# mLSTM blocks in transposed form: the gate maximum by a scan along tokens, its rows by transposing a repeated column

## The reference, cut to what matters

```python
b = jnp.cumsum(logf, axis=-1)
D = jnp.where(causal, b[..., :, None] - b[..., None, :] + logi[..., None, :], -jnp.inf)
inter = b + m[..., None]
m_t = jnp.maximum(inter, jnp.max(D, axis=-1))
w_inter = jnp.exp(inter - m_t)
S = jnp.einsum('bhtd,bhsd->bhts', q, k) * jnp.exp(D - m_t[..., None])
num = w_inter[..., None] * jnp.einsum('bhvk,bhtk->bhtv', C, q) + jnp.einsum('bhts,bhsv->bhtv', S, v)
den = w_inter * jnp.einsum('bhk,bhtk->bht', n, q) + jnp.sum(S, axis=-1)
```

## Time and profile before

| | |
|---|---|
| median of 3 runs | 2477.17 us (2476.88 to 2477.39) |
| profiled execution, its span | 2478.2 us (its time is known by the span alone) |
| PE busy | 2446.6 us |
| DVE busy | 1588.2 us |
| ACT busy | 1096.2 us |
| POOL busy | 527.5 us |
| granted TensorE clock, mean | 0.997 of full speed |
| mixer of layer 0, L1068 of block 0 to L1145 of block 8 | 191.7 to 448.1 us |
| mixer of layer 1, the same | 1410.2 to 1670.1 us |

### The profile page before, as it was taken

How to read it: one execution, slowest core, us unless ns; L and a number is a source line. 1 busy time by engine, 2 the same in 40 slices (tenths; PEclk the granted TensorE clock), 3 DMA queues, 4 the chain that set the end, 5 groups by cost and what they waited for, 6 DMA issues and landing times.

```text
span 2478.2 us, 41945 instructions
## 1 busy us (share of the span) xinstructions
PE 2446.6 (99%) x16611; PEld 2381.6 (96%) x16611; DVE 1588.2 (64%) x2693; ACT 1096.2 (44%) x2067; POOL 527.5 (21%) x490
## 2 busy tenths in 40 slices
PE   9999999999999999999999999999999999999999
PEld 8999888999999999999999988889999999999999
DVE  3115688878888887465611266878888888864564
ACT  6326656534333333343433355645334333343453
POOL 0001253423222220010110112433322222200110
PEclk9999999999999999999999999999999999999999
DMA  4442322122222223554525333212222222155564
GB/s 153 132 133 92 115 84 77 54 70 65 75 79 70 79 77 110 191 175 160 190 71 155 110 97 115 82 49 71 66 75 79 70 79 77 63 167 169 176 195 146
DMA packets 238072, 265.89 MB, mean 107 GB/s; under 512 B 15639, under 2 KB 207925, under 8 KB 235701
## 3 DMA queue, kind: packets, MB, share of 16 engines
q1 hardware_dynamic: 237876, 263.22, 33.5%
HBM read 213.06 MB, written 50.11 MB: 106 GB/s over the span
## 4 chain that ended last, share of the span: by engine, by line
PE 87%; DVE 6%; issue 3%; ACT 2%; DMA 1%; POOL 0%; SPq 0%; DVEq 0%; POOLq 0%; ACTq 0%
PE bank L323 27%; PE bank L325 26%; PE bank L324 26%; PE bank L1119 1%; PE bank L1046 1%; DMA zb<-z_scratch 1%; PE bank L1104 1%; PE bank L1088 1%; DVE actL L2265 1%; PE bank L1129 1%; PE bank L1068 1%; DVE hc L2201 0%; PE bank L1080 0%; DMA rawB<-in_w_down 0%; PE bank L999 0%
## 5 line engine op out<-in xcount | busy, mean ns | idle before, releaser
L323 PE MATMUL bank<-actH,wb 128*128 128x384 f32 (+1 forms) x1712 | 560.4, 327 | 1.8 <-DVE xT L2062 1.8
L324 PE MATMUL bank<-actL,wb 128*128 128x384 f32 (+1 forms) x1712 | 554.8, 324 | 0.0
L325 PE MATMUL bank<-actH,wb 128*128 128x384 f32 (+1 forms) x1712 | 554.4, 324 | 0.0
L323 PE MATMUL bank<-wzH,actH 128*128 128x256 f32 (+3 forms) x1296 | 369.1, 285 | 3.2 <-DVE wzL L2019 2.1
L325 PE MATMUL bank<-wzH,actL 128*128 128x256 f32 (+3 forms) x1296 | 364.2, 281 | 0.0
L324 PE MATMUL bank<-wzL,actH 128*128 128x256 f32 (+3 forms) x1296 | 363.8, 281 | 0.0
L323 PEld LDWEIGHTS bank<-actH,wb 128*128 128x128 f32 x1712 | 322.4, 188 | 7.2 <-issue 6.2
L324 PEld LDWEIGHTS bank<-actL,wb 128*128 128x128 f32 x1712 | 323.1, 189 | 0.7
L325 PEld LDWEIGHTS bank<-actH,wb 128*128 128x128 f32 x1712 | 323.2, 189 | 0.0
L323 PEld LDWEIGHTS bank<-wzH,actH 128*128 128x128 f32 (+1 forms) x1296 | 236.3, 182 | 6.1 <-issue 4.0
L323 PE MATMUL bank<-tH,wb 128*128 128x384 f32 x704 | 237.0, 337 | 1.2 <-ACT vn L1817 1.2
(11 more groups left out here) (311 smaller groups left out, 5152.5 us busy)
## 6 DMA issues: line engine op xcount, KB each, us to landing
raw<-in_w_up SPq DMA_DIRECT2D x88, 512.0 KB, 4.4
raw<-in_w_down SPq DMA_DIRECT2D x88, 512.0 KB, 3.6
g_scratch<-cv SPq DMA_DIRECT2D x44, 545.0 KB, 3.2
rawz<-in_w_in SPq DMA_DIRECT2D x22, 1024.0 KB, 5.4
zb<-z_scratch SPq DMA_DIRECT2D x16, 1156.0 KB, 5.4
tHf<-g_scratch SPq DMA_DIRECT2D x88, 192.0 KB, 3.7
z_scratch<-zst SPq DMA_DIRECT2D x128, 128.0 KB, 1.7
raw<-in_w_out SPq DMA_DIRECT2D x128, 128.0 KB, 2.8
```

The lines of the kernel that those rows point to most:

```text
L323: pe.matmul(out, aH, bH, start=first, stop=False)
L324: pe.matmul(out, aH, bL, start=False, stop=False)
L325: return pe.matmul(out, aL, bH, start=False, stop=last)
```

## The change

The mask is now that of the upper triangle, and Am, the weights and the scores stand as (s, t) instead of (t, s). The running maximum of a is no longer a reduction of a masked 128x512 matrix: PE transposes aa to four rows (`gate_rows`), DVE scans them along the tokens (`run`), PE transposes the result back to a column (`gate_columns`, between the two halves of the scores of nx), and DVE takes the maximum with mp (`gate_top`, behind the reciprocal and ahead of hc). In the next block PE spreads M_t over the partitions by transposing the column cm repeated 128 times, four transposes in place of the matmul of dA. DVE's subtraction makes mask minus M_t, ACT adds a_s as the bias of four exponentials, and the product with q by k gives WTs at once: Wt, its transposes on PE and their copy on ACT go, and so do dA on POOL and the two reductions and the subtraction on DVE.

```diff
-    t[:, CM:CM + P] = np.where(np.tril(np.ones((P, P))) > 0, 0.0, -BIG)
+    t[:, CM:CM + P] = np.where(np.triu(np.ones((P, P))) > 0, 0.0, -BIG)
...
+                def gate_rows(nx):
+                    par, i, zi, r, kind = nx
+                    pe.wait_ge(S["aa_r"], l * 9 + i + 1)
+                    if kind == "sample":
+                        pe.wait_ge(cn_r, l * 2 + 2)
+                    small(r)
+                    pe.transpose(bank[3][0:4, 8:8 + r], aa[0:r, :], ident[0:r, 0:r]).then_inc(S["aT_r"], 1)
+                def gate_columns(nx):
+                    par, i, zi, r, kind = nx
+                    pe.wait_ge(S["run_r"], l * 9 + i + 1)
+                    small(r)
+                    pe.transpose(bank[3][0:r, 136:140], run[0:4, 0:r], ident[0:4, 0:4]).then_inc(S["top_r"], 1)
...
                         if c:
-                            pe.wait_ge(S["bb_r"], b1)
+                            gate_columns(nx)
                             settle(pe, settled)
                         for p in range(4):
+                            if c and p == 2:
+                                pe.wait_ge(S["cm_r"], b1)
...
+                    if kind == "sample":
+                        gate_columns(nx)
...
-                    pe.wait_ge(S["dA_r"], b1)
+                    pe.wait_ge(S["cm_r"], b1)
...
-                    pe.matmul(bank[6][:, 0:4 * r], ones[0:r, :], dA[0:r, 0:4 * r], start=True, stop=True).then_inc(S["A_r"], 1)
+                    for h in range(4):
+                        m = pe.transpose(bank[6][:, h * P:h * P + r], cm[0:r, h:h + 1].broadcast_to([r, P]), ident[0:r, 0:r])
+                    m.then_inc(S["A_r"], 1)
...
-                        m = pe.matmul(bank[6][0:r, h * P:h * P + r], qz[:, h, 0:r], ckT[:, h // 2, 0:r],
+                        m = pe.matmul(bank[6][0:r, h * P:h * P + r], ckT[:, h // 2, 0:r], qz[:, h, 0:r],
...
-                    pe.wait_ge(S["W_r"], b1)
-                    small(r)
-                    for h in range(4):
-                        m = pe.transpose(bank[6][0:r, h * P:h * P + r], Wt[0:r, h, 0:r], ident[0:r, 0:r])
-                    m.then_inc(S["WT_r"], 1)
...
                         pe.matmul(bank[6][0:r, h * 65:h * 65 + 65], WTs[0:r, h, 0:r], Vx[0:r, h, :], start=True, stop=True)
+                    if nx is not None:
+                        gate_rows(nx)
...
+                    act.wait_ge(S["D_r"], b1)
+                    for h in range(4):
+                        t = act.activation(Am[0:r, h, 0:r], Am[0:r, h, 0:r], ACT.Exp, bias=aa[0:r, h:h + 1])
+                    t.then_inc(S["P_r"], 1)
                     act.wait_ge(S["sm_r"], b1)
                     act.activation(ex[:, :], sm[:, :], ACT.Exp).then_inc(S["ex_r"], 1)
-                    act.wait_ge(S["D_r"], b1)
-                    act.activation(Am[0:r, :, 0:r], Am[0:r, :, 0:r], ACT.Exp).then_inc(S["P_r"], 1)
...
-                    act.wait_ge(S["WT_r"], b1)
-                    act.activation(WTs[0:r, :, 0:r], bank[6][0:r, :].rearrange("p (s t) -> p s t", s=4)[:, :, 0:r],
-                                   ACT.Copy).then_inc(S["WTs_r"], 1)
...
-                        pool.wait_ge(S["aa_r"], n1)
-                        pool.tensor_tensor(dA[0:r, 0:4 * r].rearrange("p (h s) -> p h s", h=4),
...
+                    dve.wait_ge(S["aT_r"], n1)
+                    dve.tensor_tensor_scan(run[0:4, 0:r], bank[3][0:4, 8:8 + r], ones[0:4, 0:r], -3.0e38,
+                                           ALU.max, ALU.mult).then_inc(S["run_r"], 1)
+                def gate_top(nx):
+                    par, i, zi, r, kind = nx
+                    dve.wait_ge(S["top_r"], l * 9 + i + 1)
+                    dve.tensor_tensor(cm[0:r], bank[3][0:r, 136:140], mp[1 if kind == "sample" else 0][0:r],
+                                      ALU.max).then_inc(S["cm_r"], 1)
...
-                    link(dve.tensor_tensor(Am[0:r, :, 0:r], A[0:r],
-                                           table[0:r, TM:TM + r].rearrange("p (o s) -> p o s", o=1).broadcast_to([r, 4, r]), ALU.add))
-                    dve.tensor_reduce(cm[0:r], Am[0:r, :, 0:r], AX.X, ALU.max)
-                    flag(dve.tensor_reduce(G[:, :], A, AX.X, ALU.max), S["A_used"], b1)
-                    dve.tensor_tensor(cm[0:r], cm[0:r], mp[g][0:r], ALU.max)
-                    link(dve.tensor_tensor(G[:, :], G[:, :], mp[g][:, :], ALU.max))
+                    dve.scalar_tensor_tensor(Am[0:r, :, 0:r], A[0:r, :, 0:r], -1.0,
+                                             table[0:r, TM:TM + r].rearrange("p (o t) -> p o t", o=1).broadcast_to([r, 4, r]),
+                                             ALU.mult, ALU.add).then_inc(S["D_r"], 1)
+                    flag(dve.tensor_copy(G[:, :].rearrange("p (h o) -> p h o", o=1), A[:, :, r - 1:r]), S["A_used"], b1)
...
-                    dve.tensor_tensor(Am[0:r, :, 0:r], Am[0:r, :, 0:r], row(cm[0:r], 4, r), ALU.subtract).then_inc(S["D_r"], 1)
...
-                    dve.tensor_tensor(Wt[0:r, :, 0:r], bank[6][0:r, :].rearrange("p (s t) -> p s t", s=4)[:, :, 0:r],
-                                      Am[0:r, :, 0:r], ALU.mult).then_inc(S["W_r"], 1)
+                    dve.tensor_tensor(WTs[0:r, :, 0:r], bank[6][0:r, :].rearrange("p (s t) -> p s t", s=4)[:, :, 0:r],
+                                      Am[0:r, :, 0:r], ALU.mult).then_inc(S["WTs_r"], 1)
...
                     link(dve.reciprocal(dn[0:r], dn[0:r]))
+                    if nx is not None:
+                        gate_top(nx)
                     h4 = hc[0:r].rearrange("p (h d) -> p h d", h=4)
```

More of the change, by code:

```diff
@@ L227, in build @@
             aa = sb("aa", [P, 4], c=c)
-            dA = sb("dA", [P, 4 * P], c=c)
+            run = sb("run", [4, P], c=c)
             Am = sb("Am", [P, 4, P], c=c)
@@ L234, in build @@
             exk = sb("exk", [P, 4], c=c)
-            Wt = sb("Wt", [P, 4, P], c=c)
             WTs = sb("WTs", [P, 4, P], c=c)
@@ L295, in build @@
         z_in = [z_in0, z_in1]
-        MIX = ("rope_r qp_r tC_r tU_r tB_r ax_r ax_e lg_r lf_r cum_r bb_r aa_r dA_r A_r A_used sm_r ex_r exk_r D_r P_r "
-               "qk_r nd_r W_r WT_r WTs_r vss_r vms_r rv_r vn_r bq_r kT_r cT_r mix_r mA_r int_r hc_r hT_r eo_e eo_l eo_r "
+        MIX = ("rope_r qp_r tC_r tU_r tB_r ax_r ax_e lg_r lf_r cum_r bb_r aa_r aT_r A_r A_used sm_r ex_r exk_r D_r P_r "
+               "qk_r nd_r run_r top_r WTs_r vss_r vms_r rv_r vn_r bq_r kT_r cT_r mix_r mA_r int_r hc_r hT_r eo_e cm_r eo_r "
                "kw_r kwmm_r cn_up pv_r hA_r hB_r hC_r vx_r keepk_r keepv_r blk_done").split()
@@ L1555, in out_gate @@
                     act.activation(eo[0:r], z[0:r, C_O:C_O + 256], ACT.Exp, scale=-1.0).then_inc(S["eo_e"], 1)
-                    act.wait_ge(S["eo_e"], b1)
-                    act.activation(eo[0:r], eo[0:r], ACT.Ln, bias=1.0).then_inc(S["eo_l"], 1)
-                    act.wait_ge(S["eo_l"], b1)
+                    act.wait_ge(S["eo_e"], 2 * b1 - 1)
+                    act.activation(eo[0:r], eo[0:r], ACT.Ln, bias=1.0).then_inc(S["eo_e"], 1)
+                    act.wait_ge(S["eo_e"], 2 * b1)
                     act.activation(eo[0:r], eo[0:r], ACT.Exp, scale=-1.0).then_inc(S["eo_r"], 1)
@@ L1946, in mixer @@
                         pool.tensor_tensor(rv[0:r], vss[0:r], mhalf[0:r, 0:1], ALU.pow).then_inc(S["rv_r"], 1)
-                        pool.wait_ge(S["aa_r"], n1)
-                        pool.tensor_tensor(dA[0:r, 0:4 * r].rearrange("p (h s) -> p h s", h=4),
-                                           ident[0:r, 0:r].rearrange("p (o s) -> p o s", o=1).broadcast_to([r, 4, r]),
-                                           aa[0:r].rearrange("p (h o) -> p h o", o=1).broadcast_to([r, 4, r]),
-                                           ALU.mult).then_inc(S["dA_r"], 1)
                     if b is not None:
@@ L2147, in back @@
                     dve.wait_ge(S["A_r"], b1)
-                    A = bank[6][:, 0:4 * r].rearrange("p (h s) -> p h s", h=4)
-                    link(dve.tensor_tensor(Am[0:r, :, 0:r], A[0:r],
-                                           table[0:r, TM:TM + r].rearrange("p (o s) -> p o s", o=1).broadcast_to([r, 4, r]), ALU.add))
-                    dve.tensor_reduce(cm[0:r], Am[0:r, :, 0:r], AX.X, ALU.max)
-                    flag(dve.tensor_reduce(G[:, :], A, AX.X, ALU.max), S["A_used"], b1)
-                    dve.tensor_tensor(cm[0:r], cm[0:r], mp[g][0:r], ALU.max)
-                    link(dve.tensor_tensor(G[:, :], G[:, :], mp[g][:, :], ALU.max))
+                    A = bank[6][:, :].rearrange("p (h t) -> p h t", h=4)
+                    dve.scalar_tensor_tensor(Am[0:r, :, 0:r], A[0:r, :, 0:r], -1.0,
+                                             table[0:r, TM:TM + r].rearrange("p (o t) -> p o t", o=1).broadcast_to([r, 4, r]),
+                                             ALU.mult, ALU.add).then_inc(S["D_r"], 1)
```

(3 more changed lines are left out.)

## The result

Over 13 runs of each kernel, the changed kernel takes 2482.52 us (median; 2479.26 to 2484.95) and the kernel before 2477.17 (2473.66 to 2479.61). The ratio is 1.0021, 95% interval 1.0013 to 1.0028: 5.3 us slower by the medians, a little more than the 0.2% called measurable. The prediction had 2474.7 and put 0.14 on this side.

The account below looks back on a forecast made before the run. PE, busy 99% of the span, was taken to bound the kernel. Gains in most mixer blocks against +4.1 between block 2's scores and block 3's L1104 summed to -2.5 from 2477.17: 2474.7 us, range 2468.5 to 2483.

Parts of the forecast that it names:

- What queues behind it in block 2: Behind gate_top, L2044 comes 3.2 us later, then w_out and zb loads; L1104 of block 3 later by 3.2 and 0.9.
- the prediction's own signs of being wrong: Wrong if block 3's two L1104 waits don't grow, PE waits on cm, or a repeated-column transpose takes over 0.2.
- the first rival: The late zb load behind block 2 doesn't reach PE, so the 4.1 falls away: 2470.6, or 2469; 25%.
- -1.9+4.1+0.4: Block 2 up to its scores -1.9, from there to block 3's L1104 +4.1, rest of block 3 +0.4, both layers.
- The port collision stays: DVE's L2196 still held beside POOL: +0.3 six times in blocks 4 to 6, +1.7 twice in block 3; 2479.9; 12%.
- PE stands in the scores because gate_top is held: POOL holds gate_top, so PE waits between the two pairs of the second scores: +6.2 a layer, 2487; 8%.
- Blocks 0 and 1: Each block -0.52 dA matmul, -0.43 Wt transposes, +0.22 gate transposes, +0.6 CN wait: -0.13, four times, -0.5.
- Blocks 4 to 6: Gate work -0.52+0.22 = -0.3 a block, six times, -1.8; their waits another -2.0.
- its -2.0: Waits at L1104 in blocks 4 to 6 fall from 1.4 to 0.9: -2.0 for both layers, bounds 0 and -3.5.
- The sample: Block 8 has half-size tiles and half the gain: -0.4 twice, -0.8.
- the first front: The first front of a layer: +0.2 twice, +0.4.
- The half clock: Granted clock at 0.50 for 3.4 us behind the 1.88 idle, about 1.6 lost; layer 1 keeps it, 1.6 in range.

Follow-up runs that it names:

- Experiment 2: Changed kernel, but in block 2 DVE does slot 6 (the low half of the last w_in set) ahead of gate_top; 2476.37 us, ratio 0.9989.
- experiment 3: Kernel before with one wait added: in blocks 0 to 2 DVE waits ahead of hc for the first half of nx's scores; 2487.19 us, ratio 1.0030.
- experiment 1: Changed kernel, but in blocks 0 to 2 gate_top stands behind CN and slot 6, just ahead of maxima; 2474.47 us, ratio 0.9986.
- the second execution: Kernel before, unchanged, profiled once more for a second trace (also called before again); 2477.90 us.
- experiment 5: Changed kernel with the edits of experiment 1 and Experiment 4 together; 2470.70 us, ratio 0.9976; a second time, in another session, 2471.27 us, ratio 0.9974.
- Experiment 4: Changed kernel, but in block 3 POOL waits for cm_r ahead of its low half of w_out; 2481.79 us, ratio 1.0013.
- experiment 8: Version of experiment 5 with four transposes of WTs put back on PE, results unused; 2474.75 us, ratio 0.9994.
- 6: Changed kernel, but in blocks 0 to 2 PE gives gate_columns right behind the kw products, with gate_top still ahead of hc; 2474.10 us, ratio 0.9994.

## Why the prediction was wrong, step by step

**The step that failed** is "What queues behind it in block 2". The prediction named L2044 as queued behind gate_top and gave its delay rightly (3.2 us; it now starts 3.4 behind the scores' start, as against 0.2), but followed it only to SP: the w_out loads and the zb load behind them. It didn't ask who reads this low half first. That is PE, in slot 0 of block 3, the product directly behind L1162. In before's trace, layer 0 (DVE, then PE), the low half ends at 287.48 and that product starts at 287.94, so the slack was 0.5; of a delay of 3.2, less this and less the 0.6 by which PE itself was forecast later, 2.1 are left, which is what block 2 lost. Experiment 2 takes this one instruction out from behind the wait and gets back the whole of block 2; experiment 3 makes the same hole in the old kernel. Two of the prediction's own signs of being wrong are there: the waits of block 3 that it named didn't grow as it said, and PE waits on cm.

```profile
285.19 2.29 DVE L2044 TENSOR_TENSOR wzL<-rawz,wzH 128x2048 fp32r<-128x2048 f32 x1
```

```profile
287.94 0.37 PE L323 MATMUL bank<-wzH,actH 128*128 128x256 f32 x1
```

The slip that the prediction did follow is there, and costs next to nothing in after. Against the start of block 2's scores the zb loads go out 3.3 and 3.0 later than in the earlier trace rows, and POOL starts later too, but PE has been delayed by 2.1 or more by then, and L1119 of block 3 idles 0.69 and 0.76 us, not 1 to 5; 0.69 is what it idles in experiments 1 and 2 as well, where the low half isn't late. Timelines of SP, POOL and PE in after (layer 0's load, layer 1's load and its reader, then both L1119):

```profile
295.64 0.34 SPq L689 DMA_DIRECT2D zb<-z_scratch  x1
...
1516.35 0.34 SPq L689 DMA_DIRECT2D zb<-z_scratch  x1
...
1523.18 0.53 POOL L1945 TENSOR_TENSOR rp<-zb,table 128x160 f32<-128x160 f32 x1 [14.64 <-DMA zb<-z_scratch]
...
308.26 0.44 PE L1119 MATMUL bank<-CN,qz 128*128 128x65 f32 x2 [0.69 <-ACT pT L1622]
...
1526.99 0.55 PE L1119 MATMUL bank<-CN,qz 128*128 128x65 f32 x3 [0.76 <-ACT pT L1622]
```

So the first rival (the slip doesn't reach PE) was right of this path in both executions of after, but by luck in part: in layer 1 the way from POOL's start to L1119 is 3.81, as short as the 3.79 of the earlier trace rows, and POOL started 6.8 behind the load's issue. Had it taken the 8.95 of the earlier trace rows, L1119 would have come 2.1 later (an estimate from these rows), and in experiment 3 a late load did reach PE. That the forecast's +4.1 agrees with the measured +4.2 (2.1 in each layer, and 1.5 of half clock besides) is chance: it came by another path. By the prediction's own terms blocks 2 and 3 were to bring -1.9+4.1+0.4, so +2.6, and they brought +8.5: 4.2 and 1.5 in block 2, 2.8 in block 3. Besides, the forecast took the 1.88 idle and its half clock, 3.25 us, as part of every run of before, and the second execution shows that they aren't.

**Block 3**: "The port collision stays" had 12%. It was left out of the sum. Its size was +1.7 in a layer; measured are 1.42 (29.97 against experiment 5's 28.55). It put L2196 at 1.4 to 1.5 behind the kw products and POOL's add at 1.45, and took it that DVE would be ahead. DVE did come even sooner (1.32, 315.56 against 314.24; 1.56 in before), but POOL came sooner as well: its split starts 1.23 behind the kw products, and its copies ahead of it are shorter (vprev takes 0.29 where it took 0.49), presumably as vn isn't beside them any longer. Both had gained, and the order stayed. Experiment 4 shows that this order is the whole of block 3's loss. In blocks 4 to 6 L2214 is held too (0.93), yet cm comes 2.49 behind the kw products, before PE asks for it, so the +0.3 of that rival isn't there.

**PE stands in the scores because gate_top is held**: no. gate_top, with one operand in PSUM, takes 0.16 in every block, also beside POOL's adds; PE stands there because L2214 ahead of gate_top is held.

**Blocks 0 and 1** were near in the sum, 0.0 measured for -0.13, and three terms were off by 0.1 to 0.2 each. The four transposes of a repeated column take 0.53 to the next instruction, for the matmul's 0.95 in the earlier trace rows (first fence below: PE, block 0 of layer 0), so -0.42 for -0.52. They step by 0.11 as forecast, but L1094 starts 0.20 behind the last of them; the dA matmul paid the same 0.09 ahead of L1073, and the prediction had set it against transposes with another successor. gate_rows adds 0.09 between L1119 and the kw products, for 0.11. gate_columns adds 0.30, for 0.11: in experiment 1, where no wait stands, the scores take 3.05 from their start to L1162 (second fence: PE, block 1 of layer 0), for 2.75 in the earlier trace rows. The transposes of Wt are worth 0.43 to 0.45 (experiment 8), and the wait for CN 0.49 (3.54 against that 3.05), for 0.6.

```profile
192.22 0.60 PE L1088 MATMUL bank<-ident,cm 128*128 128x128 f32 x4
192.75 0.33 PE L1094 MATMUL bank<-gwT,vn 128*64 128x128 f32 x2
```

```profile
250.23 1.52 PE L1063 MATMUL bank<-kTw,bqT 64*64 64x192 f32 x16
...
253.28 0.44 PE L1162 MATMUL bank<-ident,hc 128*128 128x128 f32 x2
```

**Blocks 4 to 6**: predicted -3.8 for both layers, measured -2.1 against before's own profile (163.7 against 165.8): -0.5 to -1.0 in block 4, about -0.3 in block 5, nothing in block 6. The waits for pT are longer by their row (7.2 for 6.0, and for 4.5 in the second execution of before), since the transposes of Wt, which filled part of them, are gone; that these were worth nothing there was right. What the prediction meant by its -2.0, the way from the prob transposes to L1104 with everything in it, did shrink: over the six blocks from 8.1 to 5.4, to the 0.9 a block that it forecast, so by 2.8. The mis-sized term is the gate work: it was to bring -0.52+0.22 in each block and brought +0.1, as the row of transposes gives 0.42, gate_columns takes 0.36 with what PE stands for cm, and the stretch with gate_rows is 0.1 to 0.3 longer. **Block 7**: -0.77 in each layer, for -0.2. **The sample**: nothing, for -0.4 in each layer. Together blocks 4 to 8 came to -3.6 where the prediction has -4.6 with the first front.

**The half clock** was left out of the sum and put in the range. It followed one in two of the new idles of after (and of experiments 3 and 4, so four of eight), some 0.8 in each layer on average. That it stays away behind waits up to 1.1, as the prediction had it, was read from one trace: before again has it behind nothing longer than 0.58.

Put together, against before without its chance losses: blocks 0 and 1 0.0, block 2 +4.2 and the clock +1.5, block 3 +2.8, blocks 4 to 8 -3.6 to -3.7, in all +4.9, and 5.3 was measured. From the forecast's -2.5 that is 7.4 away: 5.9 in blocks 2 and 3, 0.5 in blocks 0 and 1, 1.0 in blocks 4 to 8. That the result lies inside the range of 2468.5 to 2483 is due to the width taken for other things (a late load, the collision), not to the term that decided.

## What to carry to other kernels

When a new wait enters an in-order queue, list every instruction behind it and for each its nearest reader on every engine, the bottleneck engine first, with the slack it had; a slot's product that is written "later" in the code may be the very next thing that PE does. Place a wait behind what others need and ahead of what only it needs, or have its producer deliver earlier: both were worth the same here. And take one late landing in one profile for a chance, not for a term: a second execution is the cheapest check of a row on which 3 us hang.

## What the runs showed of the hardware that was not expected

A DVE instruction of four elements from two SBUF operands took 0.16 alone, 0.93 beside POOL's add and 2.27 beside POOL's 128x1024 split: in both cases it was issued 0.09 us behind the start of POOL's instruction and ended with it, within 0.03. So its cost was what was left of POOL's instruction. Freeing DVE by 0.9 us left the collision in place, because POOL's split started earlier too (1.23 for 1.45 behind the kw products). The case of 0.93, DVE then POOL, block 4 of layer 0 in after:

```profile
344.13 0.93 DVE L2214 TENSOR_TENSOR dn<-dn,ex 128x4 f32<-128x4 f32 x1
```

```profile
344.04 2.14 POOL L370 TENSOR_TENSOR acc<-acc,sqn 128x384 f32<-128x384 f32 x2
```

Transposes with a stationary column repeated with step zero follow one another at 0.11, as ordinary ones do; the 0.53 for four holds 0.09 ahead of L1094 that the matmul of dA paid as well ahead of the same products. One transpose of 4 columns between the two halves of the scores cost 0.30, not the 0.15 from its start to the next start. The scan of 128 elements on 4 partitions, from PSUM, takes 0.41, and 0.28 for the 64 of block 8. The difference makes 0.26 for 128 elements and 0.15 of fixed part, which is near the prediction's estimate of 0.27 plus a fixed part.

An idle of 1.8 us in the middle of full work was followed by half clock in some places and not in others of the same execution; where it came it cost 1.5. Half clock also came behind an idle of 1.32 (experiment 5, second time) and behind none above 0.58 (before again), while in the mixers of experiments 1, 2, 6 and 8 it didn't come at all. What decides it isn't shown.
